# Output product by token tile, norms of the tiles interleaved with it, and the hidden-input turns and first weight sums moved, in one encoder layer

## The reference

```python
u = rms_norm(h, g_pre_mix); proj = u @ w_in
o_a, o_b, o_c = stick-breaking attention, recurrent block, window attention of proj's columns
mixed = concat(rms_norm(o_a, ga), rms_norm(o_b, gb), rms_norm(o_c, gc))   # 256 + 512 + 256 wide
y = mixed @ w_out                       # the mixing product
h = h + rms_norm(y, g_post_mix)         # norm of every token
u = rms_norm(h, g_pre_mlp)
f = square(relu(u @ w_ff_in)); y = f @ w_ff_out     # 1024 -> 4096 -> 1024
h = h + rms_norm(y, g_post_mlp)
```

## Time and profile before

| | us |
|---|---|
| median of 3 runs (lowest, highest) | 1162.07 (1160.93, 1162.46) |
| the profiled execution, its own time | 1161.97 |
| its span in the profile | 1160.2 |
| PE busy in the span | 1082.9 |
| DVE, ACT, POOL busy | 808.4, 573.5, 76.1 |

### The profile page before, as it was taken

One profiled execution on the slowest core, in us unless ns is written; L12 is line 12 of the kernel. 1 busy time (PEld: TensorE's weight loads), 2 busy tenths in 40 slices (PEclk: granted clock), 3 DMA queues, 4 the chain that ended last, 5 costly groups with the idle time before them and its releaser, 6 DMA issues.

```text
span 1160.2 us, 12115 instructions
## 1 busy us (share of the span) xinstructions
PE 1082.9 (93%) x4844; PEld 845.5 (73%) x4844; DVE 808.4 (70%) x767; ACT 573.5 (49%) x705; POOL 76.1 (7%) x69
## 2 busy tenths in 40 slices
PE   6999999987899999838999999999999999999993
PEld 5877777876535458737888888878888878888782
DVE  2536657655454545777778777789876799867998
ACT  6313533357464640376665546653456543466353
POOL 0004113201101000400000000000000000000000
PEclk9999999978899999978999999999999999999997
DMA  7211112110000023060130310301303003016003
GB/s 220 78 45 37 37 37 73 36 38 1 1 1 1 20 102 114 37 236 1 37 109 1 109 37 21 125 1 37 109 1 114 31 19 127 1 43 248 1 1 145
DMA packets 44624, 70.44 MB, mean 61 GB/s; under 512 B 10228, under 2 KB 19736, under 8 KB 44568
## 3 DMA queue, kind: packets, MB, share of 16 engines
q1 hardware_dynamic: 43528, 69.66, 17.7%
q10 hardware_dynamic: 1040, 0.00, 0.1%
...
## 4 chain that ended last, share of the span: by engine, by line
PE 84%; DVE 8%; ACT 4%; issue 2%; DMA 1%; DVEq 0%; ACTq 0%
PE ps L648 25%; PE ps L652 25%; PE ps L650 25%; PE ps L864 2%; PE ps L724 1%; PE ps L877 1%; PE ps L787 1%; PE ps L892 1%; PE ps L832 1%; DVE sb_e L1663 1%; ACT sb_e L1233 1%; DVE out_gained L1888 1%; DMA g_pre_mix_c<-in_g_pre_mix 1%; ACT sb_w L1213 1%; DVE ps L1697 1%
## 5 line engine op out<-in xcount | busy, mean ns | idle before, releaser
L648 PE MATMUL ps<-a_op,b_op 128*128 128x512 f32 x448 | 175.9, 393 | 5.4 <-DVE b_op L1805 4.5
L648 PE MATMUL ps<-b_op,a_op 128*128 128x512 f32 x448 | 174.6, 390 | 2.7 <-issue 2.7
L650 PE MATMUL ps<-a_op,b_op 128*128 128x512 f32 x448 | 175.6, 392 | 0.0
L652 PE MATMUL ps<-a_op,b_op 128*128 128x512 f32 x448 | 175.4, 392 | 0.0
L652 PE MATMUL ps<-b_op,a_op 128*128 128x512 f32 x448 | 174.3, 389 | 0.0
L650 PE MATMUL ps<-b_op,a_op 128*128 128x512 f32 x448 | 174.3, 389 | 0.0
L648 PE MATMUL ps<-act_hi,w_hi 128*128 128x512 f32 x288 | 115.0, 399 | 3.2 <-DVE w_lo L1455 3.2
L1805 DVE TENSOR_TENSOR b_op<-wq,b_op 128x1024 fp32r<-128x1024 f32 x96 | 116.9, 1218 | 0.0
L1347 ACT CAST a_op<-f 128x1024 fp32r<-128x1024 f32 x56 | 58.8, 1049 | 116.0 <-PE ps L652 75.7
L652 PE MATMUL ps<-act_hi,w_lo 128*128 128x512 f32 x288 | 112.8, 392 | 0.0
L650 PE MATMUL ps<-act_lo,w_hi 128*128 128x512 f32 x288 | 112.6, 391 | 0.0
...
## 6 DMA issues: line engine op xcount, KB each, us to landing
...
h_back<-h_spill SPq DMA_DIRECT2D x1, 4096.0 KB, 15.5
...
```

The costliest lines, as they stand in the source:

```text
L648: nc.tensor.matmul(dst, stat[0], mov[0], start=first, stop=False, skip_group_check=chained)
L650: nc.tensor.matmul(dst, stat[0], mov[1], start=False, stop=False, skip_group_check=chained)
L652: return nc.tensor.matmul(dst, stat[1], mov[0], start=False, stop=last, skip_group_check=chained)
```

## The change

1. The pairs of the second part go in another order (`OUT_ORDER`): tiles 0 and 1 with g = 2, then with g = 3, and from tile 2 on both halves of a tile one after the other. ACT rounds the weights of g = 3 ahead of the group root, and DVE splits them behind the first pair.
2. Tiles are normed in sets (0,1), (2,3), (4,5), (6), (7), the first three between pairs; h gets its next root in sets (0..3), (4,5), (6), (7). GpSimd makes all 8 gain products, two buffers of two tiles going round.
3. Half 0's turns use banks 0 to 3, and four of them stand ahead of the last pair. P1's first operand half is made before tile 6 is normed.
4. SP loads `wq21` when the first part is done and `wq22` when the mixing product is done, and `wq12` behind the last store of h. T1 and T2 are made by DVE ahead of half 1's turns; before they stood behind them.
5. `ut`, `h_back`, `y_gained` and `out_gained` are split into two tensors and put elsewhere, and `a_op` takes its slots from the other end, so that the earlier writes find free memory.

The diff, cut to its core:

```diff
-        ut = at("ut", [P, 2, KD, BANK], ACT_AT + 32 * K)
-        h_back = at("h_back", [P, TOK, D], ACT_AT + 32 * K)
+        ut = (at("ut0", [P, KD, BANK], X_AT + 16 * K), at("ut1", [P, KD, BANK], ACT_AT + 48 * K))
+        h_back = (at("h_back0", [P, 4, D], X_AT + 16 * K), at("h_back1", [P, 4, D], ACT_AT + 48 * K))
...
-        TILE_SETS = ((0, 1), (2, 3), (4, 5), (6, 7))
-        N_SETS = len(TILE_SETS)
+        MIX_SETS = ((0, 1), (2, 3), (4, 5), (6,), (7,))
+        MLP_SETS = ((0, 1, 2, 3), (4, 5), (6,), (7,))
+        RSQRTS = (("mix", 0), ("mix", 1), ("mlp", 0), ("mix", 2), ("mix", 3), ("mix", 4),
+                  ("mlp", 1), ("mlp", 2), ("mlp", 3))
+        def rsqrt_count(of, j):
+            return 2 + RSQRTS.index((of, j))
+        def mix_count(i):
+            return rsqrt_count("mix", min(i // 2, 3) + (i == TOK - 1))
+        OUT_ORDER = ((0, 2), (1, 2), (0, 3), (1, 3)) + tuple((s, g) for s in range(2, TOK)
+                                                             for g in (2, 3))
+        def mixed(i):
+            return 2 * TOK + 2 * (OUT_ORDER.index((i, 3)) + 1)
...
             sp.wait_ge(carry_added, adds(len(SB) - 1))
             sp.dma_start(wq11[:, :, :], block_of(0, 0, 0)).then_inc(wq_loaded[0], 16)
+            sp.wait_ge(y_ready, 2 * TOK)
+            sp.dma_start(wq21[:, :, :], block_of(0, 1, 0)).then_inc(wq_loaded[2], 16)
             for i in range(TOK):
+                if i == 6:
+                    sp.wait_ge(y_ready, Y0)
+                    sp.dma_start(wq22[:, :, :], block_of(0, 1, 1)).then_inc(wq_loaded[3], 16)
                 sp.wait_ge(h_ready, i + 1)
-                sp.dma_start(h_dram[P * i:P * (i + 1), :], y[:, i, :]).then_inc(h_stored[i // 4], 16)
-                if i == 3:
-                    sp.dma_start(wq21[:, :, :], block_of(0, 1, 0)).then_inc(wq_loaded[2], 16)
-                if i == 7:
-                    sp.dma_start(wq12[:, :, :], block_of(0, 0, 1)).then_inc(wq_loaded[1], 16)
-                    sp.dma_start(wq22[:, :, :], block_of(0, 1, 1)).then_inc(wq_loaded[3], 16)
+                sp.dma_start(h_dram[P * i:P * (i + 1), :], y[:, i, :]).then_inc(h_stored[i], 16)
+            sp.dma_start(wq12[:, :, :], block_of(0, 0, 1)).then_inc(wq_loaded[1], 16)
...
-            for i in range(TOK - 1):
-                pool.wait_ge(y_added, banks_out(3) + 2 * (i + 1))
-                nc.gpsimd.tensor_tensor(y_gained[:, i, :], y[:, i, :], rs_row[:, :], ALU.mult)\
-                    .then_inc(y_gain_done, 1)
+            pool.wait_ge(w_lo_ready, 2 * (N_IN + N_OUT))
+            for i in range(TOK):
+                pool.wait_ge(y_added, mixed(i))
+                if i >= 4:
+                    pool.wait_ge(h_ready, i - 3)
+                nc.gpsimd.tensor_tensor(y_gained[i // 2 % 2][:, i % 2, :], y[:, i, :], rs_row[:, :],
+                                        ALU.mult).then_inc(y_gain_done, 1)
...
-            for g in range(2, N_OUT):
-                slot = (N_IN + g) % 2
-                pe.wait_ge(w_lo_ready, 2 * (N_IN + g + 1))
-                for s in range(TOK):
-                    n = banks_out(g) + 2 * s
-                    if n == 2 * TOK:
-                        pe.wait_ge(o_copied, 4)
-                    for i, k in enumerate((2, 0)):
-                        pe.wait_ge(mix_lo, 6 + 2 * i)
-                        pe.wait_ge(y_added, n + i - 3)
-                        token_major(slot, act_hi, act_lo, s, (k, k + 1), bank_out(n + i),
-                                    first=k, last=k + 1).then_inc(y_ready, 1)
...
-            def turn_hidden_inputs(half):
+            def turn_hidden_inputs(half, ks):
                 pe.wait_ge(hn_ready, 4 * (half + 1))
-                for k in range(KD):
+                for k in ks:
                     t = KD * half + k
                     if t < 4:
-                        pe.wait_ge(y_added, Y0 - 3 + t)
+                        pe.wait_ge(grp_var, 3)
+                    elif half and k < 4:
+                        pe.wait_ge(y_added, Y0 - 3 + k)
...
-                        mm = nc.tensor.transpose(ps[:, 4 + t % 4, P * i:P * (i + 1)],
+                        mm = nc.tensor.transpose(ps[:, 4 * half + t % 4, P * i:P * (i + 1)],
...
+            for e, (s, g) in enumerate(OUT_ORDER):
+                n = 2 * TOK + 2 * e
+                if e == 0:
+                    pe.wait_ge(o_copied, 4)
+                if s == 0:
+                    pe.wait_ge(w_lo_ready, 2 * (N_IN + g + 1))
+                for i, k in enumerate((2, 0)):
+                    pe.wait_ge(mix_lo, 6 + 2 * i)
+                    pe.wait_ge(y_added, n + i - 3)
+                    token_major((N_IN + g) % 2, act_hi, act_lo, s, (k, k + 1), bank_out(n + i),
+                                first=k, last=k + 1).then_inc(y_ready, 1)
+                if e == 0:
+                    group_sums(2, 0, work[:, 4, :])
+                if e == len(OUT_ORDER) - 2:
+                    turn_hidden_inputs(0, range(4))
+            turn_hidden_inputs(0, range(4, KD))
...
-                    elif kk == 0 and n == 1:
-                        pe.wait_ge(ut_by_act, KD)
-                        pe.wait_ge(ut_by_dve, KD)
+                    elif kk == 0:
+                        pe.wait_ge(ut_by_act, KD // 2 * (n + 1))
+                        pe.wait_ge(ut_by_dve, KD // 2 * (n + 1))
...
-            turn_hidden_inputs(0)
...
-                        turn_hidden_inputs(1)
+                        turn_hidden_inputs(1, range(KD))
...
+            split_hi(N_IN + 3, (N_IN + 1) % 2)
             group_rsqrt(2)
-            split_hi(N_IN + 3, (N_IN + 1) % 2)
...
-            def mix_squares(j):
-                tiles = TILE_SETS[j]
-                act.wait_ge(y_added, banks_out(3) + 2 * (tiles[-1] + 1))
...
+            def mix_squares(i):
+                act.wait_ge(y_added, mixed(i))
+                squares(i, work[:, 5, :])
...
-            for j in range(3):
-                mix_squares(j)
+            mix_squares(0)
+            mix_squares(1)
+            mix_root(0)
+            mix_squares(2)
             h_squares(0)
+            h_squares(1)
             mix_squares(3)
-            act.wait_ge(y_ready, Y0)
-            normed(0)
-            turned(0)
-            round_operands(0)
-            h_squares(1)
-            normed(1)
-            round_operands(1)
-            turned(1)
+            mix_root(1)
+            mix_squares(4)
+            h_squares(2)
+            h_squares(3)
+            mlp_root(0)
+            mix_squares(5)
+            mix_root(2)
+            for i in range(4):
+                normed(i)
+            mix_squares(6)
+            mix_root(3)
+            turned(0, (0, 2))
+            round_operands(0, [0])
+            turned(0, (4, 6))
+            mix_squares(7)
+            mix_root(4)
+            h_squares(4)
+            h_squares(5)
+            mlp_root(1)
+            round_operands(0, [1])
+            normed(4)
+            normed(5)
+            h_squares(6)
+            mlp_root(2)
+            round_operands(1, [0])
+            h_squares(7)
+            mlp_root(3)
+            normed(6)
+            normed(7)
+            turned(1, (0, 2, 4, 6))
+            round_operands(1, [1])
             def late_squares(i, c, total):
                 n_squares[0] += 1
...
+                    gained = y_gained[i // 2 % 2][:, i % 2, :]
+                    dve.wait_ge(y_gain_done, i + 1)
+                    nc.vector.scalar_tensor_tensor(
+                        out=y[:, i, :], in0=gained, scalar=rstd[:, i:i + 1],
+                        in1=x_again[:, i, :] if i < 4 else work[:, i - 4, :],
+                        op0=ALU.mult, op1=ALU.add).then_inc(h_ready, 1)
...
-                    if g == 3 and s % 2 and s > 1:
-                        norm_mix(s // 2 - 1)
-                    if g == 2 and s == 4:
-                        split_lo(N_IN + 3, (N_IN + 3) % 2)
-            rsqrt(slice(0, 4), 5)
-            dve.wait_ge(rows_loaded, 16)
-            dve.wait_ge(y_added, Y0)
-            gain_last(y_gained, rs_row[:, :])
-            norm_mix(3)
...
-            turned(0)
-            rest_operands(0)
-            rsqrt(slice(4, TOK), 7)
-            rest_operands(1)
-            turned(1)
+            dve.wait_ge(rows_loaded, 16)
+            mix_rows(0)
+            split_lo(N_IN + 3, (N_IN + 3) % 2)
+            for j in range(3):
+                for e in range(4 * j + 1, 4 * j + 5):
+                    if e == 12:
+                        mlp_root(0)
+                    mix_rows(e)
+                mix_tiles(j)
+            mix_rows(13)
+            mix_rows(14)
+            turned(0, (1, 3))
+            mix_rows(15)
+            turned(0, (5, 7))
+            rest_operands(0, [0])
+            mix_tiles(3)
+            rest_operands(0, [1])
+            mix_tiles(4)
+            mlp_root(1)
+            mlp_root(2)
+            block_sum(0, "T1")
+            mlp_root(3)
```

(7 more changed lines are left out.)

161 lines of the change are left out of this document (78 added, 83 removed).

## The result

| | before | after |
|---|---|---|
| median, us (lowest to highest, runs) | 1162.13 (1160.93 to 1162.46, 4) | 1147.67 (1143.23 to 1148.60, 4) |
| ratio, 95% interval | | 0.9873 [0.9858, 0.9888] |
| profiled execution: own time, span | 1161.97, 1160.2 | 1147.69, 1146.0 |
| PE, DVE, ACT, POOL busy | 1082.9, 808.4, 573.5, 76.1 | 1080.7, 805.1, 574.7, 78.5 |

The kernel is faster by 14.5 us in the medians. The sign was right, and so was the chain of waits up to P2; what the forecast had wrong begins with P2's length.

The account below looks back on a forecast made before the run. PE's waits and lower clock before P2, 28.9 us, were taken as the bound. P2 starting at 525.4 instead of 536.62 gives 11.2 us, less 0.8: 1161.97 - 10.4 = 1151.6 us, range 1148 to 1156.5.

Parts of the forecast that it names:

- the chain of waits up to P2: From the mixing product's second part to P2: the 14.9 us stop goes, P1 starts at 499.3, P2 at 525.4.
- P2's length: P2 was to take 12.5 us from a lower-clock start, ending at 537.9, with P6's operands ready at 535.9.
- The stop and the norms: Mixing product to P1: norms fit between pairs, 14.9 us stop gone, new 1.8 us wait at third pair, P1 at 499.3.
- Tiles 6 and 7, T1's wait: Behind P1's start: T1 waits for wq12, a 6.4 us load, until 513.1; tile 7 is scaled at 517.2.
- Half 1's turns: Ahead of P2: eight turns at 0.9 us each and 1.0 for the last bank, so P2 starts at 525.4.
- The allowance: 0.8 us taken off the gain, since the same layout put P2 of before at 535.1, 1.5 us short of the trace.
- The sum: P2's start moves from 536.62 to 525.4, 11.2 us; less 0.8, a gain of 10.4 us.
- The larger gain: Rival, chance 0.10: wq12 lands in 4.9 us and turns run at 0.65; P2 near 522.8, gain 13, time 1149.
- The wait for wq12: Rival, chance 0.04: slower, as the load ahead of T1 takes over 16.8 us; at 20 us the time is 1165.2.
- the two places counted: DVE instructions waiting for GpSimd's products: 1.8 us at h's first root, 0.4 at a_op; more meetings belonged to a 0.22 rival.
- given back in stage 0: Rival, chance 0.04: P6 or the products behind it start no earlier, since DVE's sums set them; 1161.6, no change.

Follow-up runs that it names:

- late_load: The changed kernel with wq12 issued only when the last store of h has landed; 1148.35 us, 0.9887 of before.
- sums_back: The changed kernel with T1 and T2 put back behind half 1's turns; 1153.33 us, 0.9927 of before.
- filled_stop: The changed kernel with four matmuls of unused result added on PE behind P1, ahead of half 1's turns; 1147.35 us, 0.9875 of before.
- the best version: The changed kernel with roots reordered on ACT and DVE and P2's first operand half rested ahead of T1; 1143.17 and 1143.16 us, 0.9840 and 0.9841 of before.
- before_filled: The kernel before with one matmul of unused result added ahead of each of half 1's eight turns; 1164.78 us, 1.0025 of before.
- order_alone: The kernel before with only the order of pairs changed, norms of the first three sets between them; 1154.61 us, 0.9938 of before.
- sums_alone: The kernel before with only T1 and T2 moved, behind the root of h of tiles 4 to 7; 1162.05 us, 0.9997 of before.
- order_sums: The kernel before with the order of pairs changed and T1 and T2 moved too; 1154.45 us, 0.9936 of before.
- early_root: The changed kernel with tiles 4 and 5's root of h earlier on ACT and DVE, tile 7's norm before P1's second operand half; 1144.67 us, 0.9857 of before.
- early_rests: The changed kernel with early_root's order and P2's first operand half rested by DVE ahead of T1; 1143.17 us, 0.9840 of before.

## Why the prediction was right, and where it fell short

*The stop and the norms.* Right. The new wait at the third pair is 1.6 us (1.8 forecast), PE waits for no rows behind it, the last pair is done near 492.7 (493.2), and P1 starts at 499.45 (499.3) behind a rest that waited for GpSimd until 497.1 (496.8).

*Tiles 6 and 7, T1's wait.* Right, step by step: second operand at 501.5 (501.9), tile 7's norm at 504.6 (505.0), the load issued at 506.3 (506.6) and T1 released by DMA at 512.8 (513.1), the scaling's end at 516.9 (517.2). Counted from the third pair, which itself came 0.6 us early, each of these is within 0.3 us of the layout. P1 took 13.65 us where I gave it 12.6, which cost nothing: PE still waited 3.6 us behind it (some 5 forecast). late_load and sums_back show that T1 with its wait is on this chain.

*Half 1's turns.* A term mis-sized. I took 0.9 us each and 1.0 for the last bank, 8.2; they took 6.28 and 0.94, 7.2. The clock rose at 522.2 with nothing but turns on PE since 517. By the rule of the Trainium skill, TensorE: Matmul & The Clock Gate, Part 4 (PE-mode transpose), they would all have been at half clock. The trace does not agree with it for half 1 in the kernel after, and in filled_stop and the best version the clock was 1.00 through all of them. My sentence that the trace of before agrees for half 1's turns misreads it too: four of the eight took 1.91 us, full clock by my own price, and the clock fell only at 533.2, among the last ones. The page speaks of a transpose mode; the records, plain MATMUL rows, don't show which mode these were in.

*P2's length, the step that failed.* "P2 at the lower clock 12.5 us": I carried the 12.48 us of the earlier trace rows over and let the gain be P2's start alone. P2 took 10.94. The text had the right numbers beside each other (T1 and T2 gone from behind P2, 0.4 us to spare at P6 if P2 ran at full clock; measured 0.3) and drew nothing from them. The runs show two conditions that only work together. From P2's start to the end pass 623.6 us with the sums behind P2 and P2 slow (before) or fast (before_filled, order_alone), 623.7 with the sums moved and P2 slow (sums_alone), and 621.8 with the sums moved and P2 fast (after, order_sums). Before, P2's start at half clock cost nothing, because DVE's operands for P6 were there only at 549.15, just when P2 ended:

```profile
547.93 1.22 DVE L1805 TENSOR_TENSOR b_op<-wq,b_op 128x1024 fp32r<-128x1024 f32 x1
...
549.25 0.47 PE L648 MATMUL ps<-a_op,b_op 128*128 128x512 f32 x1
```

The change took that second limit away, and the half clock too, whose spell now ends within the turns. Worth 1.7 us.

*The allowance.* I took off 0.8 us because my layout gave P2 of before 1.5 too early. No such shortfall came after: from the third pair to the scaling's end the layout had 64.2 us, and they took 64.5. That the shortfall before was the slow clock in that kernel's last turns is likely, but no run shows it.

*The sum.* Forecast 10.4. Added: 0.56 upstream, 0.7 for the turns with the small differences ahead of them, 0.8 for the allowance, 1.7 for P2 with P6: 14.2, which is the difference of the spans. P2 is the largest term, but no term alone leaves the range: with P2's the forecast would have been 1149.9, with the allowance and the turns 1148.4, and only the 0.56 us from upstream, which this change did not make, take it below 1148. *Rivals.* The larger gain came (0.10 forecast), mostly by another cause than the one given (the turns gave 0.7 us of it), and with a load of 6.4 us, not 4.9. The wait for wq12 did not decide, DVE met GpSimd's products at the two places counted (1.5 and 1.1 us for 1.8 and 0.4), and nothing was given back in stage 0.

Open: what decides in one run whether a stop brings a slow spell. early_root with a stop of 2.8 us and sums_back with 2.7 had one; the best version, with 2.6 and 1.8 us in its two profiles, had none. So the 2 us that early_rests gained beyond its expectation may in part be luck of the clock, the same in both profiles. No run varied the stop alone.
